# Work reordered at five places of a two-block kernel: affine steps, column sums, low parts, a broadcast, and the last two up projections

## The reference

```python
z = h @ w_in; u, v, g = split(z, 3)              # gated MLP mixer, width 2048
v = layer_norm(v, ln_g, ln_b)
sv = einsum('gts,bcsgd->bctgd', tril(ws), v) + bs  # 16 groups of 128
y = (u * sv * silu(g)) @ w_out
...
p = softmax(q @ k_band.T + sink); o = p @ v_band   # banded attention
y = (o * silu(g)) @ w_out
...
mod = silu(c) @ ada_w + ada_b                      # 6 x 1024 column sums
h = rmsnorm(x) * (1 + sc1) + sh1                   # second block, attention
x = x + g1 * y
h2 = rmsnorm(x) * (1 + sc2) + sh2
x = x + g2 * peer(h2)      # top 16 of 128 x 128 keys, 8 heads; a = gelu(h2 @ u), y = (gates * a) @ v
out = rmsnorm(x, final_g)
```

## Time and profile before

| | us |
|---|---|
| median of 3 runs | 1311.07 |
| lowest and highest | 1310.95, 1311.61 |
| the profiled execution | 1311.91 |
| its span, first to last instruction | 1310.2 |
| PE busy | 1276.3 (97%) |
| DVE busy | 984.7 (75%) |
| ACT busy | 761.3 (58%) |
| POOL busy | 390.4 (30%) |

### The profile page before, as it was taken

One profiled execution on the slowest core, in us unless ns is written; L12 is line 12 of the kernel. 1 busy time (PEld: TensorE's weight loads), 2 busy tenths in 40 slices (PEclk: granted clock), 3 DMA queues, 4 the chain that ended last, 5 costly groups with the idle time before them and its releaser, 6 DMA issues.

```text
span 1310.2 us, 26231 instructions
## 1 busy us (share of the span) xinstructions
PE 1276.3 (97%) x8596; PEld 1166.1 (89%) x8596; DVE 984.7 (75%) x1849; ACT 761.3 (58%) x1292; POOL 390.4 (30%) x254
## 2 busy tenths in 40 slices
PE   7989999999999989999999999999999999999997
PEld 7989998898999989999999988888888888888885
DVE  6999988897987767978889765556666666666666
ACT  6444454556766555458888645445555555555554
POOL 1179913225060347887777400000000000000000
PEclk9999999999999989999999999999999999999999
DMA  9977776453766344553333455555765565566652
GB/s 368 340 240 252 256 252 222 153 174 115 262 217 200 103 168 156 180 182 128 115 113 114 128 193 184 187 190 185 247 192 186 185 188 183 188 189 192 189 186 73
DMA packets 69344, 248.15 MB, mean 189 GB/s; under 512 B 7968, under 2 KB 8352, under 8 KB 68512
## 3 DMA queue, kind: packets, MB, share of 16 engines
q1 hardware_dynamic: 59920, 213.04, 49.5%
q10 hardware_dynamic: 9360, 34.27, 7.7%
HBM read 244.66 MB, written 2.62 MB: 189 GB/s over the span
## 4 chain that ended last, share of the span: by engine, by line
PE 73%; DVE 2%; ACT 1%; issue 1%; POOL 1%; ACTq 0%; DVEq 0%; POOLq 0%
PE ps L2483 26%; PE ps L1915 18%; PE ps L2494 10%; PE ps L2496 5%; PE ps L2454 4%; PE ps L2323 1%; PE ps L2198 1%; PE ps L2086 1%; POOL tmp L1854 1%; PE ps L2065 1%; PE ps L2105 1%; PE ps L2395 1%; PE ps L2075 1%; ACT WH L498 0%; PE ps L2532 0%
## 5 line engine op out<-in xcount | busy, mean ns | idle before, releaser
L1016 DVE TENSOR_TENSOR WL<-raw,WH 128x1024 fp32r<-128x1024 f32 x320 | 407.3, 1278 | 85.4 <-ACT WH L498 81.7
L498 ACT ACTIVATE WH<-raw 128x1024 fp32r<-128x1024 f32 x392 | 411.4, 1053 | 64.1 <-PE ps L1915 30.1
L1915 PE MATMUL ps<-X,WH 128*128 128x256 f32 x1888 | 350.8, 287 | 1.9 <-DVE WL L1016 1.7
L1915 PEld LDWEIGHTS ps<-X,WH 128*128 128x128 f32 x1888 | 294.8, 192 | 2.7 <-DVE WL L1016 1.9
L1915 PE MATMUL ps<-X,WL 128*128 128x256 f32 x944 | 267.8, 284 | 0.0
L2494 PE MATMUL ps<-X,WH 128*128 128x512 f32 x576 | 205.6, 397 | 0.0
L1881 POOL TENSOR_TENSOR WL<-raw,WH 128x1024 fp32r<-128x1024 f32 x72 | 173.6, 2415 | 76.3 <-ACT WH L498 76.2
L2483 PE MATMUL ps<-WH,wvL 128*128 128x512 f32 x496 | 195.5, 394 | 0.0
L2483 PE MATMUL ps<-WL,wvH 128*128 128x512 f32 x496 | 195.3, 394 | 0.0
L2483 PE MATMUL ps<-WH,wvH 128*128 128x512 f32 x496 | 195.3, 394 | 0.0
L1915 PEld LDWEIGHTS ps<-X,WL 128*128 128x128 f32 x944 | 181.1, 192 | 0.0
(11 more groups left out here) (355 smaller groups left out, 2333.4 us busy)
## 6 DMA issues: line engine op xcount, KB each, us to landing
raw<-stream SPq DMA_DIRECT2D x392, 512.0 KB, 4.2
ada<-adaT ACTq DMA_DIRECT2D x47, 512.0 KB, 4.2
bias<-att_bias ACTq DMA_DIRECT2D x8, 512.0 KB, 4.8
x<-xT ACTq DMA_DIRECT2D x2, 512.0 KB, 5.8
raw<-stream SPq DMA_DIRECT2D x4, 256.0 KB, 6.1
ws<-wsT SPq DMA_DIRECT2D x1, 1024.0 KB, 8.4
lng<-rows SPq DMA_DIRECT2D x1, 1024.0 KB, 8.6
lnb<-rows SPq DMA_DIRECT2D x1, 1024.0 KB, 9.1
```

The costliest lines, as they stand in the source:

```text
L498: act.activation(WH[:, slot, :], raw[:, slot, :], ACT.Copy).then_inc(h_done, 1)
L1016: dve.tensor_tensor(WL[:, slot, :], raw[:, slot, :], WH[:, slot, :].bitcast(F32), ALU.subtract).then_inc(l_done, 1)
L1915: mm = pe.matmul(out_ap, a(kc), b(kc), start=(first and kc == 0 and i == 0), stop=(last and kc == KC - 1 and i == 2))
```

## The change

- Mixer: DVE makes the low part `lo(C_UG + 3)` after the two short normalising instructions and ahead of the two long ones. POOL makes `v_affine(2)` and `v_affine(3)` ahead of `gate_product(0)` and `gate_product(1)`; before, they alternated.
- Banded attention: DVE's column sum moves from the end of step m to just behind the gate (L1301), and one step later (tile 29+m in step m in place of 30+m). ACT's load of a column tile moves from ahead of the Tanh to the end of its step.
- Output projection: ACT makes the high part of tile 6 between the two squares of tile 5, and the chunk's high part ahead of it; DVE makes `gained_low(6)` in step 6, ahead of a chunk's low part, in place of step 7.
- Broadcast: PE makes the two products for g2 behind `token_sums` in place of ahead of `turn_x`; ACT copies them last, and the turned x of tiles 1 and 3 in the middle of `x1_high`; ACT makes the first two query copies ahead of the following high parts.
- End: DVE and ACT take the last two chunks' high and low parts between the Gelus of the last three experts in place of ahead of them; the last expert's parts are made ahead of the last but one's, and PE's last down projections use them in that order.

```diff
@@ scalar: swa_step
                 if m < 8:
-                    load_ada(31 + m, g)
                     act.wait_ge(gr_ready, up(AG + m + 1, g, 2))
                     ...
                     act.activation(th[:, m % 2, :], gr2[:, m % 2, :], ACT.Tanh).then_inc(gate_ready, 1)
                 if 1 <= m <= 8:
                     pt_out(m - 1, g, 3)
+                if m < 8:
+                    load_ada(31 + m, g)
@@ scalar: after the banded attention
-            for n in range(KC):
-                if n >= 1:
-                    hi(C_BOUT + 3 + n)
-                    gained_high(n - 1)
+            for n in range(KC - 1):
+                hi(C_BOUT + 4 + n)
+                if n < KC - 2:
+                    gained_high(n)
+                two_squares(n, (lambda: gained_high(KC - 2)) if n == KC - 3 else (lambda: None))
             gained_high(KC - 1)
+            two_squares(KC - 1)
@@ scalar: before the experts
-            act.wait_ge(tr_mm, 1)
             act.wait_ge(act_link, 2)
-            for i in range(2):
-                link.mark(act.activation(g2b[:, i * 512:i * 512 + 512], ps[:, 2 + i, :], ACT.Copy))
-            xtok_out(0, 2)
-            xtok_out(2, 3)
+            xtok_out(0, 1)
+            xtok_out(2, 2)
             ...
-            x1_high(5 * KC, mod[:, 24:32])
+            x1_high(5 * KC, mod[:, 24:32], range(4))
             xtok_out(1, 4)
             xtok_out(3, 5)
+            x1_high(5 * KC, mod[:, 24:32], range(4, KC))
+            for i in range(2):
+                link.mark(act.activation(g2b[:, i * 512:i * 512 + 512], ps[:, 2 + i, :], ACT.Copy))
             ...
-            for n in range(4):
+            qt_out(0)
+            hi(C_WQ + 3)
+            qt_out(1)
+            hi(C_WQ + 4)
+            sc_out(0)
+            for n in range(2, 4):
                 wq_step(n)
@@ scalar: the end
-            column_step(LATE - 3)
-            for i in (LATE - 2, LATE - 1):
-                gelu(i)
-                w_high(i)
+            gelu(LATE - 3)
+            w_high(LATE - 3)
+            hi(NCHUNK - 2)
+            gelu(LATE - 2)
+            hi(NCHUNK - 1)
+            gelu(LATE - 1)
+            w_high(LATE - 1)
+            w_high(LATE - 2)
@@ vector: mixer
-            for cols in (slice(0, 2 * P), slice(2 * P, AW)):
+            def scaled(cols):
                 for t in range(NT):
                     ...
+            scaled(slice(0, 2 * P))
             lo(C_UG + 3)
+            scaled(slice(2 * P, AW))
@@ vector: swa_step
                     dve.scalar_tensor_tensor(out=tiles(sgate, m - 1, g, 2), ...).then_inc(th_ready, 1)
+                    ada_tile(29 + m, g)
                 if 2 <= m <= 9:
                     o_out(m - 2, g)
                 ...
                     soft_sum(m - 1, g, True)
-                if m < 8:
-                    ada_tile(30 + m, g)
@@ vector: output projection
-                if n >= 1:
+                if 1 <= n < KC - 1:
                     gained_low(n - 1)
+                if n == KC - 2:
+                    gained_low(n)
                 if 2 <= n < KC - 1:
                     lo(C_BOUT + 3 + n)
@@ vector: the end
-            column_step(LATE - 3)
-            for i in (LATE - 2, LATE - 1):
-                gated(i)
-                w_low(i)
+            gated(LATE - 3)
+            w_low(LATE - 3)
+            lo(NCHUNK - 2)
+            gated(LATE - 2)
+            lo(NCHUNK - 1)
+            gated(LATE - 1)
+            w_low(LATE - 1)
+            w_low(LATE - 2)
@@ gpsimd: mixer
-            for n in range(2):
-                gate_product(n)
-                v_affine(n + 2)
+            v_affine(2)
+            v_affine(3)
+            gate_product(0)
+            gate_product(1)
@@ tensor: before the experts
-            pe.wait_ge(diag_ready, 1)
-            (the two products with ones, then_inc(tr_mm, 1))
             turn_x(0); turn_x(2); cout_half(7, 0); cout_half(7, 1)
             token_sums((tmp[5], tmp[0]), tmp[1], 41, 37)
+            pe.wait_ge(diag_ready, 1)
+            (the two products with ones, then_inc(tr_mm, 1))
             pe.wait_ge(x_ready, 32)
             turn_x(1)
             token_spread(7)
             ...
-            pe.wait_ge(act_link, 4)
+            pe.wait_ge(act_link, 8)
             key_scores(0)
@@ tensor: the end
-            for j in range(NK - 3, NK):
+            turned = (NK - 3, NK - 1, NK - 2)
+            for j in turned:
```

More of the change, by code:

```diff
@@ L687, in gained_high, with two_squares @@
                 act.activation(XGH[:, n, 0:T], tmp[n % 2][:, :], ACT.Copy).then_inc(xh_ready, 1)
+            def two_squares(n, between=lambda: None):
                 act.wait_ge(sacc_done, 8 + 2 * n - 1)
                 act.activation(tmp[4][:, :], x[:, n, :], ACT.Square).then_inc(sq_ready, 1)
+                between()
                 act.wait_ge(sacc_done, 8 + 2 * n)
@@ L1674, in w_low @@
             def w_low(i, g=None):
-                dve.wait_ge(wh_ready, up(EARLY + i + 1, g, 2))
+                dve.wait_ge(wh_ready, up(EARLY + i + 1 - (i == LATE - 1) + (i == LATE - 2), g, 2))
                 if i == LATE - 1:
@@ L2363, in _ @@
             pe.wait_ge(ot_done, NPAIR)
-            pe.wait_ge(diag_ready, 1)
-            for i in range(2):
-                mm = pe.matmul(ps[:, 2 + i, :], ones[:, :],
-                               diags[:, 4 * i:4 * i + 4, :].rearrange("p k n -> p (k n)"), start=True, stop=True)
-            mm.then_inc(tr_mm, 1)
             def turn_x(i):
@@ L2382, in _ @@
             token_sums((tmp[5], tmp[0]), tmp[1], 41, 37)
+            pe.wait_ge(diag_ready, 1)
+            for i in range(2):
+                mm = pe.matmul(ps[:, 2 + i, :], ones[:, :],
+                               diags[:, 4 * i:4 * i + 4, :].rearrange("p k n -> p (k n)"), start=True, stop=True)
+            mm.then_inc(tr_mm, 1)
             pe.wait_ge(x_ready, 32)
@@ L2528, in last_down @@
                 pe.wait_ge(l_done, c + 1)
-                pe.wait_ge(wl_ready, j + 1)
+                pe.wait_ge(wl_ready, j + 1 - (j == NK - 1) + (j == NK - 2))
                 high, low = (lastH, lastL) if j == NK - 1 else (wvH[:, j % 2, :], wvL[:, j % 2, :])
@@ L2533, in last_down @@
                                    b[:, c % RING, h * 512:(h + 1) * 512], start=False,
-                                   stop=(j == NK - 1 and i == 2), skip_group_check=True)
+                                   stop=(j == NK - 2 and i == 2), skip_group_check=True)
                 return mm
-            for j in range(NK - 3, NK):
+            turned = (NK - 3, NK - 1, NK - 2)
+            for j in turned:
                 for h in range(2):
```

## The result

The changed kernel takes 1313.82 us (median of 20 executions, 1312.03 to 1316.81), the kernel before 1311.68 (20 executions, 1310.93 to 1313.40). The ratio is 1.0015, 95% interval 1.0008 to 1.0022: about 2.0 us slower (1.0 to 2.9). The forecast was 1313.1, that is 2.05 over the kernel before. So sign and size came out, but of the five terms two held, one was too small, and two that this trace confirms did not come out when they were made alone. The profiled execution took 1314.24 us, its span is 1312.0.

What follows compares the result with a forecast made beforehand. PE, busy nearly throughout, was taken as the bound, its waits the only time to win. Terms -1.3+4.6+0-1.5+0.25 = +2.05 us took the median from 1311.07 to 1313.1 us, range 1308.3 to 1315.6.

Steps and rivals of the forecast that it cites:

- five terms: Mixer -1.3, column sums +4.6, output projection 0, broadcast -1.5 and end +0.25 us, together +2.05.
- What bounds the kernel, and where to look: Whole kernel: PE is busy nearly throughout, so reordering wins only at its waits; check clock and other engines there.
- Column sums: Banded attention: the sum ahead of gr lengthens the DVE-ACT loop from 9.42 to 10.5 us; +4.6 us.
- first rival: Banded attention: moved column sums cost nothing, only 0.4 us for the rotary sum is gained; 1308.1 us, chance 0.17.
- Mixer: Early low part and affine steps: up to 6.1 us gained at PE's waits, only 1.3 gets through DVE's backlog; -1.3.
- starting 0.8 late: Mixer: POOL's early passes slow DVE's low parts, so DVE starts 0.8 us late and just catches up by stage end.
- 1.3 us wait for the last low part of y: Mixer's end: PE arrives earlier but waits about 1.3 us for DVE's last low part of y.
- 1.5 of 6.1 us: Mixer: share of the upper-bound gain that comes from avoiding the half-clock stretch behind the 2.9 us wait.
- Output projection: Output projection: last low part 0.3 us later, hidden under PE's wait for POOL's additions; 0, bounds -0.3 and +0.3.
- Broadcast: Broadcast of g2: norm chain 0.5 us earlier and the first query copy 1.0 sooner behind it; -1.5 us.
- The clock at 0.57 costs nothing extra here: Broadcast: low clock over 462 to 470 us adds no time, because DVE's and ACT's chain ends last.
- The end: Last experts: last expert's low part 1.15 us earlier, last but one's 1.35 later; PE ends at 1297.8 against 1297.5, +0.25.

Runs made afterwards that it cites:

- trial of the two other places: Kernel before with only the column sum moved: behind the attention's output on, 1317.18 us (ratio 1.0049); right behind gr, 1312.26 us (1.0008).
- short sums: Changed kernel with column sums and loads put back, each mixer column sum over 64 of 1024 columns: 1307.57 us, ratio 0.9974 to the kernel before.
- first experiment: Changed kernel with column sums and their loads put back, other four edits kept: 1309.85 us, ratio 0.9984 to the kernel before.

## Why the prediction was right, point by point

**What bounds the kernel, and where to look.** This held. PE's waits and the fill of the engine behind each place gave the signs of all terms in a trace with a high clock.

**Column sums, +4.6; measured +4.3 in the traces, 4.0 by putting them back, 5.2 alone.** The mechanism held in each detail named ahead: 10.42 us per step for 10.5, 1.58 of idle time for 1.6, the line at turn_out with 4.4 for 3 to 5, POOL's sum at 0.73. The trial of the two other places shows that gr, not on, carries it. The division among the steps was off: in the trace of the sums alone PE loses 0.7 us in step 3 (0.6 forecast), 2.6 in steps 4 to 6 (3.4), 1.1 in step 7, for which I had named nothing, and 0.2 in step 8 (0.65). That the total came out is partly luck. The first rival (the sums are free, by the Trainium skill's rule in "SBUF — State Buffer", section "SBUF: two separate sides") falls, though the rule's premise agrees with the rows: POOL's 1.82 became 0.73. DVE's own sum took 1.23 beside POOL and 1.22 alone; what the rule promised came to POOL, which had 3.6 us of idle time to spare.

**Mixer, -1.3; measured -2.25.** Too small by 1.0. The step that failed is "starting 0.8 late": I let DVE keep the 0.8 us that POOL's early passes cost it. It does start late (81.46 less 0.89 of start is 80.57, for 80.8 forecast), but its next step is 5.3 us long in place of 6.06, because POOL is idle beside its low parts (1.23 and 1.21 below), and at 86.75-0.89 = 85.9 it is already ahead of the earlier trace rows:

```profile
81.46 1.23 DVE L1033 TENSOR_TENSOR WL<-raw,WH 128x1024 fp32r<-128x1024 f32 x1 [0.56 <-ACT WH L498]
...
82.94 1.21 DVE L1033 TENSOR_TENSOR WL<-raw,WH 128x1024 fp32r<-128x1024 f32 x1
...
86.75 1.76 DVE L1033 TENSOR_TENSOR WL<-raw,WH 128x1024 fp32r<-128x1024 f32 x1
```

PE's wait for a low part near 82 us came as forecast, with 1.2. The 1.3 us wait for the last low part of y never came; 0.7 at the last copy of u came in its place. That DVE's backlog takes part of the gain was right; the short sums show it, with POOL relieved beside it. What the argument had the wrong way round is what the gain consists of: I counted the clock as 1.5 of 6.1 us, of which the backlog keeps most. The traces in which the clock holds without the edit show that it is nearly all of the gain. So the gain should be absent in some executions, which fits the 0.65 by the ratio for the edit alone.

**Output projection, 0; +0.08 where the clock holds, +1.44 in the trace of it alone.** The order of the work came out as told (last low part later, POOL's wait gone). What was missed is that two waits merge into one of 2.3 us. My own text had the two points, a clock that fell behind 2.9 us and not behind 1.7, used them for the mixer and did not ask the same of the other four places.

**Broadcast, -1.5; -1.74 where the clock holds, 0 alone.** The sum of 0.5 and 1.0 was nearly right, and so was its first part: less the 3.1 us that PE is late at 450 us, the norm's spread comes 0.45 earlier. "The clock at 0.57 costs nothing extra here" was right of the old order only; the edit itself put 1.9 us of PE's work on the path at that place.

**The end, +0.25; measured +0.27.** The new wait for lastL is 1.5 (1.9 forecast), and PE ends as worked out.

**The sum.** On the traces: too little gain in the mixer (1.0) and at the broadcast (0.2), 0.3 too much loss at the sums. So the terms of this trace give +0.7 where I had +2.05. Against that stand low stretches of the clock, of some 1.7 us each: the 20 executions go from a mean clock of 0.999 and 0.998 (medians 1312.7 and 1312.85) to 0.997 and 0.996 (1313.94 and 1314.68), with one at 0.994 (1316.81). At the high clock the kernel is 1.0 over the kernel before, at the low one 2.7, and the forecast lies between. So two errors of opposite sign, the terms and the clock, meet in the median, and the total was right partly by that luck. The profiled execution can't show this: it has no such stretch and is slow for other reasons, start and rest above all.

**What stays open.** The edits' times don't add up: broadcast alone 0.0, output projection and end +1.7, affine steps -0.65, yet these together (first experiment) -2.1. Each of these figures has an interval of about 1.2 to either side, so part of the gap of 3.1 can be spread. Whether the clock falls at one place seems to hang on what came earlier; no run here shows the rule. I also can't say at which place the slower executions of the changed kernel have their low stretch: there is one trace for each kernel, and this one has none.

## What to carry to other kernels

Small work moved into another engine's shadow is free only as long as it stands behind the instruction that others wait for: look for the first instruction of the loop's chain (here gr), not for the one that PE's list of waits names. When a reorder merges waits of PE or moves PE's work onto the path, ask whether the clock falls there, and put the moved work where nobody waits for it even at the lower level. For differences of 1 or 2 us take the mean clock of each execution beside its time, and don't trust a ledger made of two traces.

## What the runs showed of the hardware that I had not expected

A single wait of 2.3 us of PE was followed by a fall to the lower clock in one kernel's trace and not in three others with the same wait at the same place. The start varies too: PE does 44, 36 or 46 matmuls in the window from 10 to 16 us in three traces with no edit there, which shifts all that follows by up to 1 us. DVE's column sum and POOL's addition beside each other slow only POOL (1.82 to 0.73 when apart), not the sum (1.23 and 1.22), while the low part, also on DVE, takes 1.76 to 1.78 beside POOL and 1.22 alone.
